# A fused two-block model on one core: product groups opened differently, waits per tile, and three reorderings behind the expert stage

## The chip, the cores and the metric

The kernel runs on 1 core of one Trainium2 chip. Its engines work beside each other: TensorE (PE, matrix products; its weight loads are listed as PEld), VectorE (DVE), ScalarE (ACT), GpSimd (POOL) and SyncE (SP, which here only issues DMAs). They meet by semaphores: an instruction waits until a counter has reached a value. The metric is the time on the device in microseconds, as the median of several runs. All data is fp32, at batch 1, 256 tokens and a model width of 1024.

## The reference

Two blocks one after the other on x (256 x 1024), cut to what matters here:

```python
# first block
z = rmsnorm(x, g_mix) @ w_in                      # pool mixer, short convolution, gates
x = x + m @ w_out
x = x + peer_ffn(rmsnorm(x, g_ffn), ...)          # 8 heads x top 16 of 16384 experts: gathers
x = rmsnorm(x, g_final)
# second block, layer 0 (gated linear attention) and layer 1 (sparse attention)
for i in range(2):
    xn = rmsnorm_2(h, norm_mix[i])
    main = gla_mixer(...) if i == 0 else nsa_mixer(...)
    mo = mem_attention(mq, mem_kv)                # 4 memory heads
    h = h + concatenate([main, mo]) @ w_out[i]
    h = h + conv_ffn(rmsnorm_2(h, norm_ffn[i]), ...)  # up 1024 -> 2 x 2816, convolution over 3 tokens, silu(a) * b, down
return rmsnorm_2(h, final_norm)
```

rmsnorm divides by sqrt(mean(x^2) + 1e-6) and multiplies by a gain per channel.

## The kernel before

Activations lie transposed, 128 channels on the partitions, 8 tiles (k = 0..7) of 256 tokens. One product in the code is 128 x 128 by 128 x 256 and is two fp32 matmul instructions. Products go into four rotating PSUM banks (`bank`) in an order written down in the list GROUPS; `begin` waits until the bank's former user has been taken out by ACT or DVE (`freed`). A second PSUM area, `wide`, is four banks that hold attention scores, the heads' outputs or the FFN's sum. Weights stream through a ring of four slots in SBUF (`wring`): SP issues a load when the group that last used the slot is complete, and `slot` makes PE wait for it. Every engine runs its instructions in the order in which its part of the program is written; nothing reorders them.

What the change and the next sections touch, in the order of the program:

- **Output projection of layer 0, `wout0`.** Four tiles of two output rows, each a sum over eight input tiles, n = 0..7: first the two of the memory heads (`moT`), then six of the attention (`gout`). DVE makes those head by head (L1566 to L1576: a reciprocal, products, a gated product) and counts them in `g_out`, for which PE waits product by product. The loop is `for i in range(4): for n in range(KT): wout0(i, n)`: a tile is finished before the next begins. Each tile is then added to x by DVE (L1267), squared by ACT and folded by POOL (L514) for the norm's mean.
- **FFN, `ffn`, once in each layer.** PE first writes zeros to all of `wide` with four matmuls on a zero tile (L2293), so that every down product can add. Up-projections 0 and 1 take the weighted x before the norm's scale is known (`raw`, L1817); the mean of squares (L1829) is made inside the first, ACT makes the root, DVE the reciprocal into `rstd` (L1136), scales up-projection 0 (L1142) and makes the eight normed tiles hT = x * gain * rstd (`finish`, L1147), then scales up-projection 1. Up-projection 2 and all later ones use hT; PE waits for all eight tiles in front of it (`pe.wait_ge(normed, norms)`). Tiles from 3 on are made with seven products instead of eight, from sums that POOL makes: four of the weights (`weight_sums`, L530 to L535) and, once, four of hT (`hidden_sums`, L543 to L548, waiting for all eight tiles). After up 2, `down(0, 0)` adds the first hidden tile into `wide` (L2354); it waits for DVE's product (L1608). The loop then alternates an up tile and a down tile.
- **Sparse attention of layer 1.** For each pair of heads PE makes scores, DVE adds the bias and takes the maximum (`nsa_max`, L1744), ACT the exponentials (L1045), DVE the probabilities (`nsa_probs`, L1754 to L1763), PE transposes them (L2443), ACT copies the transposes out (`nsa_turned`), PE makes the values. Before the loop DVE makes four maxima and then the probabilities of the first pair. ACT's queue is exponentials 0 to 3, then the copies of transposes 0 and 1, then exponentials 4 and 5.
- **Final norm.** ACT squares x in four pieces, PE makes the mean (L1807), ACT the root (L663), DVE the reciprocal, in place in PSUM (L1117), and eight products with x and the gain (L1121). SP stores two tiles at a time (L489).

## Time and profile before

| | |
|---|---|
| runs, median (lowest to highest of 3) | 1591.55 us (1589.33 to 1594.05) |
| profiled execution | 1592.82 us, its span 1591.0 us |
| busy: PE, DVE, POOL, ACT | 92%, 59%, 38%, 26% |
| mean granted clock of TensorE | 0.989 of full speed |
| mean DMA rate over the span | 264 GB/s |

The span is the time between the first and the last instruction of the profiled execution; the rest of its time lies around it. All rows of the trace belong to that one execution. A row that merges instructions gives start, duration to the end of the last one, engine, line, operation, tiles, shape and count; a bracket at its end says how long the engine had been idle and whose work ended that.

### The profile page before, as it was taken

The numbers are of one execution on the slowest core, as the hardware profiler recorded it, in microseconds if no ns is written. First come the engines' busy times: TensorE is split into PE (matmuls) and PEld (weight loads), VectorE is DVE, ScalarE is ACT, GpSimd is POOL, SyncE is SP. The second block draws the span as 40 slices with busy tenths as digits, with TensorE's granted clock in tenths as the row PEclk, the third lists the DMA queues.
The fourth block names the chain that finished last, engine by engine and source line by source line (L and its number), as shares of the span: only waits on it lengthen the run. The fifth ranks groups of instructions, "written<-read, shape, count | busy, mean of one in ns | idle before, by whom it ended". The sixth has DMA issues, their size and how long they took to land.

```text
span 1591.0 us, 21988 instructions
## 1 busy us (share of the span) xinstructions
PE 1471.1 (92%) x7682; PEld 1100.0 (69%) x7682; DVE 936.5 (59%) x2355; ACT 405.9 (26%) x990; POOL 597.3 (38%) x525
## 2 busy tenths in 40 slices
PE   8999999999899877777789999999999999999997
PEld 6998845555445433222246788999998877899997
DVE  5662587666766776676456833655554235555554
ACT  2110223212222232222214621111112235211122
POOL 4860234334434443344342303555531000455550
PEclk9999999999999999999999999999999999999999
DMA  8465699999999999999996125644534320644441
GB/s 334 160 222 184 234 427 427 427 426 427 427 423 413 425 427 427 427 414 415 426 426 211 68 103 204 231 159 158 164 143 131 106 107 1 225 159 159 158 132 40
DMA packets 63383, 420.63 MB, mean 264 GB/s; under 512 B 7340, under 2 KB 7788, under 8 KB 16812
## 3 DMA queue, kind: packets, MB, share of 16 engines
q0 software_dynamic: 38560, 277.19, 42.0%
q1 hardware_dynamic: 24736, 142.35, 25.2%
q8 instruction: 47, 0.77, 0.2%
q14 instruction: 40, 0.33, 0.1%
HBM read 417.28 MB, written 3.45 MB: 264 GB/s over the span
## 4 chain that ended last, share of the span: by engine, by line
PE 64%; DMA 20%; DVE 5%; issue 5%; POOL 3%; ACT 2%; SPq 0%; POOLq 0%; DVEq 0%
DMA arena<-uv_dram,arena 19%; PE bank L2314 15%; PE wide L2354 10%; PE wide L2109 9%; PE bank L1840 6%; PE bank L1866 5%; PE bank L1959 3%; ACT arena L663 2%; PE bank L1920 2%; POOL arena L503 2%; PE bank L2487 2%; PE bank L1930 2%; PE bank L2282 2%; PE bank L1817 2%; PE bank L2131 1%
## 5 line engine op out<-in xcount | busy, mean ns | idle before, releaser
L2109 PE MATMUL wide<-arena 128*128 128x512 f32 x1024 | 477.9, 614 | 90.7 <-ACT arena L663 90.5
L2109 PEld LDWEIGHTS wide<-arena 128*128 128x128 f32 x1024 | 191.7, 194 | 354.4 <-issue 198.5
L1386 DVE CUSTOM_DVE_ANT_0 arena<-arena,wide 128x1024 f32<-128x1024 f32 x256 | 312.5, 1221 | 189.4 <-DMA arena<-uv_dram,arena 184.3
L503 POOL DMA_INDIRECT arena<-uv_dram,arena x256 | 259.3, 1013 | 405.3 <-PE wide L2109 287.1
L663 ACT ACTIVATE arena<-arena 128x2 f32<-128x2 f32 (+4 forms) x205 | 72.2, 354 | 537.0 <-DVE arena L1386 416.5
L1600 DVE SCALAR_TENSOR_TENSOR arena<-arena,prm 128x255 f32<-128x255 f32 (+1 forms) x152 | 126.0, 850 | 55.6 <-ACT arena L663 55.5
L2354 PE MATMUL wide<-arena,wring 128*128 128x256 f32 x704 | 158.6, 379 | 0.0
L2354 PEld LDWEIGHTS wide<-arena,wring 128*128 128x128 f32 x704 | 130.9, 190 | 16.2
L1634 DVE TENSOR_TENSOR arena<-bank,arena 128x128 f32<-128x128 f32 x266 | 74.0, 290 | 105.1 <-PE bank L2314 101.5
L514 POOL TENSOR_TENSOR arena<-arena 128x512 f32<-128x512 f32 x15 | 20.2, 1350 | 262.3 <-ACT arena L663 261.6
L663 ACT ACTIVATE arena<-bank 128x128 f32<-128x128 f32 (+8 forms) x101 | 40.4, 402 | 285.3 <-PE bank L2314 104.4
L530 POOL TENSOR_TENSOR arena<-wring 128x512 f32<-128x512 f32 x38 | 48.6, 1280 | 158.5 <-PE bank L2314 153.6
L2314 PE MATMUL bank<-arena 128*128 128x128 f32 x912 | 108.0, 275 | 0.0
L2314 PEld LDWEIGHTS bank<-arena 128*128 128x128 f32 x912 | 104.9, 192 | 0.0
L663 ACT ACTIVATE arena<-cst,arena 128x128 f32<-128x128 f32 x256 | 88.8, 393 | 41.2 <-DVE arena L1407 40.2
L1840 PE MATMUL bank<-hT,wring 128*128 128x256 f32 x384 | 85.1, 381 | 2.3 <-DVE hT L1147 2.3
L1840 PEld LDWEIGHTS bank<-hT,wring 128*128 128x128 f32 x384 | 72.3, 190 | 13.3 <-DVE hT L1147 3.1
L2314 PE MATMUL bank<-hT,wring 128*128 128x128 f32 x608 | 80.2, 275 | 0.0
L2314 PEld LDWEIGHTS bank<-hT,wring 128*128 128x128 f32 x608 | 76.9, 192 | 2.0
L663 ACT ACTIVATE arena<-arena,prm 128x256 f32<-128x256 f32 x76 | 41.5, 593 | 113.9 <-DVE arena L1634 113.9
L1817 PE MATMUL bank<-arena,wring 128*128 128x256 f32 x224 | 52.1, 393 | 7.7 <-DMA wring<-win_dram 7.7
L533 POOL TENSOR_TENSOR arena<-arena,wring 128x512 f32<-128x512 f32 x38 | 54.6, 1436 | 0.0
(290 smaller groups left out, 2040.4 us busy)
## 6 DMA issues: line engine op xcount, KB each, us to landing
wring<-ffn_dram SPq DMA_DIRECT2D x43, 1024.0 KB, 5.1
wring<-ffn_dram SPq DMA_DIRECT2D x44, 512.0 KB, 3.5
wring<-win_dram SPq DMA_DIRECT2D x15, 1024.0 KB, 5.2
wring<-wout_dram SPq DMA_DIRECT2D x12, 1024.0 KB, 4.7
wring<-wq_dram SPq DMA_DIRECT2D x5, 1024.0 KB, 7.3
wring<-mix_dram SPq DMA_DIRECT2D x4, 1024.0 KB, 5.3
arena<-uv_dram,arena POOLq DMA_INDIRECT x256, 12.1
wring<-memkv_dram SPq DMA_DIRECT2D x4, 1024.0 KB, 9.3
```

The source lines that it names most:

```text
L503: pool.indirect_dma_start(out=G[:, n % NBUF, :], out_offset=None, in_=a["uv"], in_offset=bass.IndirectOffsetOnAxis(ap=idx[:, u, r:r + 1], ...
L533: TT_(s2, s1, a11, ALU.subtract).then_inc(w_sums, 1)
L663: return nc.scalar.activation(o, i, func, scale=scale, **kw)
L1386: V.tensor_tensor_reduce(out=G[:, n % NBUF, 0:D], in0=G[:, n % NBUF, 0:D], in1=wide[:, 0:2, :].rearrange("p a b -> p (a b)"), scale=1.0, s ...
L1600: return V.scalar_tensor_tensor(out=fy[:, k % 2, c, sh:S], in0=src, scalar=w_, in1=fy[:, k % 2, c, sh:S], op0=ALU.mult, op1=ALU.add)
L1634: V.tensor_tensor(o, own, i, ALU.add).then_inc(joined, 1)
L1817: ins = MM(b[:, m * S:(m + 1) * S], w[:, (m * KT + k) * 128:(m * KT + k + 1) * 128], src[:, k, :], start=k == 0 and m == 0, stop=k == KT - ...
L1840: ins = MM(b[0:rows, m * S:(m + 1) * S], w[:, (m * kt + k) * width:(m * kt + k) * width + rows], src[:, k, :], start=k == 0, stop=k == kt - 1)
L1866: ins = MM(o, a_[:, q * 128:(q + 1) * 128], b_[:, q, :], start=q == 0, stop=q == 3)
L2109: ins = MM(wide[:, 2 + h, :], diag[:, n % 4, e, :], G[:, r % NBUF, D + 512 * h:D + 512 * (h + 1)], start=r % (HEADS * TOPK) == 0, stop=r % ...
L2314: ins = MM(o, a_[:, q * 128:(q + 1) * 128], b_[:, q, :], start=q == 0, stop=q == 3)
L2354: ins = MM(wide[:, m // 2, (m % 2) * S:(m % 2 + 1) * S], w[:, (16 + m) * 128:(17 + m) * 128], fh[:, k % 2, :], start=False, stop=last and ...
```

## The change

Five edits:

1. `wout0`: the products of the two memory tiles (n = 0, 1) of all four output tiles come first, then n = 2..7 of each. PE waits for `g_out` in the first tile only.
2. FFN: the four zeroing matmuls are gone; the first down product (`first=True`) carries the start flag on the first product of each bank. The zero tile in SBUF goes with them.
3. FFN: the wait for all eight normed tiles ahead of up-projection 2 becomes one wait per tile, in its first half.
4. Sparse attention: `nsa_probs(0)` stands between the second and the third maximum in DVE's order.
5. Final norm: the reciprocal goes to `rstd` in SBUF; DVE makes tiles 0 to 4. ACT multiplies tiles 5 to 7 of x with the gain, ahead of the root, and POOL multiplies them with rstd. The stores are five: tiles 0-1, 2-3, 5-6, 4, 7.

A sixth touches one constant: the root of `mean_mix0` gets `eps2` = 1e-12 for `eps`.

```diff
--- before.py
+++ after.py
@@ -149,8 +149,8 @@
         prm = sb("prm", [128, PRM_W])
         memk = sb("memk", [128, 2, 2, S])
         memv = sb("memv", [128, 2, TT, 256])
-        zero = sb("zero", [128, 512], bf16)
         eps = sb("eps", [128, 1])
+        eps2 = sb("eps2", [128, 1])
         rstd = sb("rstd", [128, S])
         AW = 31900
         arena = sb("arena", [128, AW])
@@ -347,6 +347,7 @@
         group_full = sem("group_full")
         freed = {ACT_: sem("freed_by_act"), DVE_: sem("freed_by_dve")}
         zeroed = sem("zeroed")
+        weighted, normed_pool = sem("weighted"), sem("normed_by_pool")
         fence = {e: sem(f"fence_{e}") for e in ("pool", "dve")}
         squared = sem("squared")
         rooted = sem("rooted")
@@ -484,10 +485,11 @@
                         sp.dma_start(wq4[m], a["wq4"][:, m]).then_inc(aside_in, 16)
                 for s in range(0 if name != "win" else slots, slots):
                     load(s, s)
-            for n in range(4):
-                sp.wait_ge(normed, 8 * 10 + 2 * n + 2)
-                sp.dma_start(out[:, 2 * n:2 * n + 2, :], hT[:, 2 * n:2 * n + 2, :]).then_inc(stored, 16)
-            sp.wait_ge(stored, 64)
+            for ks, ready, count in ((slice(0, 2), normed, 82), (slice(2, 4), normed, 84), (slice(5, 7), normed_pool, 2),
+                                     (slice(4, 5), normed, 85), (slice(7, 8), normed_pool, 3)):
+                sp.wait_ge(ready, count)
+                sp.dma_start(out[:, ks, :], hT[:, ks, :]).then_inc(stored, 16)
+            sp.wait_ge(stored, 80)
 
 
         @block.gpsimd
@@ -652,6 +654,10 @@
                                    kvc[64 * base:64 * base + 64, :, 16 * half:16 * half + S - 16]).then_inc(c_moved, 16)
             fold(sqF, 20)
             sums(1, 80)
+            pool.wait_ge(weighted, 3)
+            pool.wait_ge(freed[DVE_], TAKEN[GROUP0["mean_out"]])
+            for k in range(5, KT):
+                nc.gpsimd.tensor_tensor(hT[:, k, :], xgF[:, k, :], rstd[:], ALU.mult).then_inc(normed_pool, 1)
 
 
         @block.scalar
@@ -675,10 +681,10 @@
                     act.wait_ge(wait, at[n])
                     copy(o[:, 2 * n:2 * n + 2, :], i[:, 2 * n:2 * n + 2, :], func=ACT.Square).then_inc(squared, 1)
 
-            def root(stage, i=0, rows=128, n=S):
+            def root(stage, i=0, rows=128, n=S, bias=eps):
 
                 b = full(stage, i)[0:rows, 0:n]
-                copy(b, b, func=ACT.Sqrt, bias=eps[0:rows]).then_inc(rooted, 1)
+                copy(b, b, func=ACT.Sqrt, bias=bias[0:rows]).then_inc(rooted, 1)
 
 
             act.preload_act_table(ACT.Sqrt)
@@ -841,7 +847,7 @@
             for k in range(KT):
                 act.wait_ge(added, 7 + k // 4)
                 both(1, k).then_inc(sq_done, 1)
-            root("mean_mix0")
+            root("mean_mix0", bias=eps2)
 
             def expo(J):
                 layer, kind, h, tt = JOBS[J]
@@ -1094,6 +1100,8 @@
             ffn("ffn1", 1)
             act.preload_act_table(ACT.Sqrt)
             square(sqF, xT, added, [21, 22, 23, 24])
+            for k in range(5, KT):
+                copy(xgF[:, k, :], xT[:, k, :], scale=P("final_norm", k)).then_inc(weighted, 1)
             root("mean_out")
 
 
@@ -1147,11 +1155,11 @@
                     V.scalar_tensor_tensor(out=dst[:, k, :], in0=src[:, k, :], scalar=col[:, k:k + 1], in1=rstd[:],
                                            op0=ALU.mult, op1=ALU.mult).then_inc(normed, 1)
 
-            V.memset(zero[:], 0.0).then_inc(zeroed, 1)
             for z in zp:
                 V.memset(z[:, :, 0:16], 0.0).then_inc(zeroed, 1)
             V.memset(cu[:, :, 0:2], 0.0).then_inc(zeroed, 1)
             V.memset(eps[:], EPS).then_inc(zeroed, 1)
+            V.memset(eps2[:], EPS * EPS).then_inc(zeroed, 1)
             dve.wait_ge(g_mix_in, 16)
             for k in range(KT):
                 dve.wait_ge(x_in[k // 4], 16)
@@ -1764,9 +1772,11 @@
                     ins.then_inc(n_p, 1)
 
             dve.wait_ge(late, LATE)
-            for J in range(4):
-                nsa_max(J)
+            nsa_max(0)
+            nsa_max(1)
             nsa_probs(0)
+            nsa_max(2)
+            nsa_max(3)
             for Q in range(len(NSA) // 2):
                 if 2 * Q + 2 < len(NSA):
                     nsa_probs(Q + 1)
@@ -1779,7 +1789,8 @@
             finish(hT, xT, P("norm_ffn", 8, 8))
             scale("ffn1", 1)
             ffn("ffn1", 1)
-            norm("mean_out", xT, [(hT, "final_norm", 0)])
+            inverse("mean_out")
+            finish(hT, xT, P("final_norm", 0, 8), range(5))
 
 
         @block.tensor
@@ -2272,7 +2283,7 @@
                 if n == 0:
                     begin("wout0", i)
                     slot("wout0", i)
-                if k < 6:
+                if k < 6 and i == 0:
                     pe.wait_ge(g_out, k + 1)
                 b = bank[(GROUP0["wout0"] + i) % 4]
                 w = wring[:, (SLOT0["wout0"] + i) % RING, :]
@@ -2284,19 +2295,20 @@
                     done(ins)
 
             for i in range(4):
-                for n in range(KT):
+                for n in range(2):
+                    wout0(i, n)
+            for i in range(4):
+                for n in range(2, KT):
                     wout0(i, n)
 
             def ffn(stage, layer, norms, gains, mean):
                 g0, n0, k0 = GROUP0[stage], SLOT0[stage] - layer, layer * FT
-                for n in range(4):
-                    MM(wide[:, n, :], zero[:, 0:128], zero[:], start=True, stop=False)
                 def up(j, mean=None):
                     b = begin(stage, j)
                     if layer and j == 0:
                         pe.wait_ge(front1_in, 16)
                     w = front1 if layer and j == 0 else slot(stage, j - layer)
-                    done(raw(w, xgF, b, gains, mean) if j < 2 else project(w, hT, b))
+                    done(raw(w, xgF, b, gains, mean) if j < 2 else project(w, hT, b, norms=norms - 8))
 
                 def up_seven(j, k):
 
@@ -2346,13 +2358,13 @@
                     earlier = sum((SLOT0["ffn0"] + s) % RING == r for s in range(FT)) if layer else 0
                     return 16 * (earlier + k // RING + 1)
 
-                def down(j, k, last=False):
+                def down(j, k, first=False, last=False):
                     pe.wait_ge(f_hid, j + (k0 + 1))
                     pe.wait_ge(d_full[(n0 + k) % RING], down_loads(k) if isinstance(j, int) else up_seven.i * 16 + down_loads(k))
                     w = wring[:, (n0 + k) % RING, :]
                     for m in range(KT):
                         ins = MM(wide[:, m // 2, (m % 2) * S:(m % 2 + 1) * S], w[:, (16 + m) * 128:(17 + m) * 128],
-                                 fh[:, k % 2, :], start=False, stop=last and m % 2 == 1)
+                                 fh[:, k % 2, :], start=first and m % 2 == 0, stop=last and m % 2 == 1)
                         if last and m % 2:
                             ins.then_inc(f_sum, 1)
                     if not last:
@@ -2360,9 +2372,8 @@
 
                 up(0, mean)
                 up(1)
-                pe.wait_ge(normed, norms)
                 up(2)
-                down(0, 0)
+                down(0, 0, first=True)
                 for j in range(PLAIN, 6):
                     up_seven(j, j)
                     down(j - 2, j - 2)
@@ -2372,7 +2383,7 @@
                         up_seven(i * 4 + (s + 6), s + 6)
                         down(i * 4 + (s + 4), s + 4)
                 down(FT - 2, FT - 2)
-                down(FT - 1, FT - 1, True)
+                down(FT - 1, FT - 1, last=True)
 
             ffn("ffn0", 0, 56, 16, ("mean_f0", sqF, 12))
             for i in range(2):
```

PE's order around `wout0`; bank2, bank3, bank0 and bank1 are the four output tiles, gla_out is `g_out`, w_full the ring's loads. Before:

```order
L1840 MATMUL bank1<-hT,wring 128x256 x15
L2282 MATMUL bank2<-arena,wring 128x256 [waits w_full3,freed_by_act]
L2282 MATMUL bank2<-arena,wring 128x256 x3
L2282 MATMUL bank2<-arena,wring 128x256 [waits gla_out]
L2282 MATMUL bank2<-arena,wring 128x256
```

After:

```order
L1851 MATMUL bank1<-hT,wring 128x256 x15
L2293 MATMUL bank2<-arena,wring 128x256 [waits w_full3,freed_by_act]
L2293 MATMUL bank2<-arena,wring 128x256 x3
L2293 MATMUL bank3<-arena,wring 128x256 [waits w_full0,freed_by_act]
L2293 MATMUL bank3<-arena,wring 128x256 x3
L2293 MATMUL bank0<-arena,wring 128x256 [waits w_full1,freed_by_act]
L2293 MATMUL bank0<-arena,wring 128x256 x3
L2293 MATMUL bank1<-arena,wring 128x256 [waits w_full2,freed_by_act]
L2293 MATMUL bank1<-arena,wring 128x256 x3
L2293 MATMUL bank2<-arena,wring 128x256 [waits gla_out]
```

The memory products of tiles two to four, with their waits for ring slot and bank, now stand ahead of the first wait for a head.

PE's order around the third up-projection of layer 0 (`bank<-hT,wring` behind `bank<-arena,wring`, up-projection 1). Before:

```order
L1817 MATMUL bank<-arena,wring 128x256 [waits gained]
L1817 MATMUL bank<-arena,wring 128x256
L1840 MATMUL bank<-hT,wring 128x256 [waits w_full1,freed_by_dve,normed]
L1840 MATMUL bank<-hT,wring 128x256 x15
L2354 MATMUL wide<-arena,wring 128x256 [waits d_full3,ffn_hidden]
L2354 MATMUL wide<-arena,wring 128x256 x7
```

After:

```order
L1828 MATMUL bank<-arena,wring 128x256 [waits gained]
L1828 MATMUL bank<-arena,wring 128x256
L1851 MATMUL bank<-hT,wring 128x256 [waits normed,w_full1,freed_by_dve]
L1851 MATMUL bank<-hT,wring 128x256 [waits normed] x7
L1851 MATMUL bank<-hT,wring 128x256 x8
L2366 MATMUL wide<-arena,wring 128x256 [waits d_full3,ffn_hidden]
L2366 MATMUL wide<-arena,wring 128x256 x7
```

The one wait for `normed` became eight, on the products of the first output row; the down product stands where it was.

DVE's order at the start of the sparse attention; a maximum is the ISA rows of 128x128 or 128x256, the probabilities begin with the 128x4 TENSOR_SCALAR that waits for nsa_exp. Before:

```order
L1744 ISA arena<-wide,arena 128x256
L1744 ISA arena 128x1
L1744 ISA arena<-wide,arena 128x256 [waits nsa_scores]
L1744 ISA arena 128x1
L1744 ISA arena<-wide,arena 128x256
L1744 ISA arena 128x1
L1754 TENSOR_SCALAR arena<-arena 128x4 [waits nsa_exp]
L1756 RECIPROCAL arena<-arena 128x4 [waits dve_steps]
L1759 TENSOR_TENSOR arena<-arena 128x4 [waits dve_steps]
L1763 TENSOR_SCALAR arena<-arena 128x128 [waits dve_steps]
```

After:

```order
L1752 ISA arena<-wide,arena 128x128
L1752 ISA arena 128x1
L1762 TENSOR_SCALAR arena<-arena 128x4 [waits nsa_exp]
L1764 RECIPROCAL arena<-arena 128x4 [waits dve_steps]
L1767 TENSOR_TENSOR arena<-arena 128x4 [waits dve_steps]
L1771 TENSOR_SCALAR arena<-arena 128x128 [waits dve_steps]
L1771 TENSOR_SCALAR arena<-arena 128x128 x3
L1752 ISA arena<-wide,arena 128x256 [waits nsa_scores]
```

The first probabilities moved ahead of the two maxima of 256 columns, behind the second of 128.

## Rows read from the trace of the kernel before

**Rows 1.** The page's first part: busy us, share of span, instructions.

```profile
PE 1471.1 (92%) x7682; PEld 1100.0 (69%) x7682; DVE 936.5 (59%) x2355; ACT 405.9 (26%) x990; POOL 597.3 (38%) x525
```

**Rows 2.** The chain that ended last: start us, us, engine, line, count.

```profile
1361.32 5.18 PE bank L1817 x24
```

**Rows 3.** The timeline of wout0, 944 to 1000: start, us, engine, line, operation.

```profile
950.76 4.48 PE L2282 MATMUL bank<-arena,wring 128*128 128x256 f32 x20
...
950.95 0.33 SPq L428 DMA_DIRECT2D wring<-wout_dram  x1
...
956.98 0.87 DVE L1576 SCALAR_TENSOR_TENSOR arena<-arena,prm 128x256 f32<-128x256 f32 x2
...
957.12 25.26 PE L2282 MATMUL bank<-arena,wring 128*128 128x256 f32 x108 [1.88 <-DVE arena L1572]
...
982.22 1.03 PE L2293 MATMUL wide<-zero 128*128 128x512 bf16 x4
```

**Rows 4.** Window: us; PE, PEld, DVE, ACT, POOL busy; clock, DMA share, GB/s.

```profile
958.30:961.70 3.40, 3.40 (x10) 2.68 (x9) 0.23 (x1) 0.00 (x0) 0.00 (x0) 0.51 0.00 0
```

**Rows 5.** DMA issues from 930 to 1000: count, KB each, median us to landing.

```profile
wring<-wout_dram SPq DMA_DIRECT2D x3, 1024.0 KB, 4.7
...
arena<-turned_dram POOLq DMA_DIRECT2D x1, 1536.0 KB, 15.2
```

**Rows 6.** The timeline of the first FFN's norm, 985 to 1012.

```profile
989.13 8.80 PE L1817 MATMUL bank<-arena,wring 128*128 128x256 f32 x40
...
998.80 7.17 PE L1840 MATMUL bank<-hT,wring 128*128 128x256 f32 x32 [0.88 <-DVE hT L1147]
...
1001.20 0.43 DVE L1608 TENSOR_TENSOR arena<-arena 128x256 f32<-128x256 f32 x1 [0.16 <-ACT arena L663]
...
1002.84 1.28 POOL L548 TENSOR_TENSOR arena<-hT,arena 128x512 f32<-128x512 f32 x1
...
1005.82 3.62 PE L2354 MATMUL wide<-arena,wring 128*128 128x256 f32 x16
```

**Rows 7.** The timeline of the second FFN's norm, 1345 to 1400.

```profile
1360.30 1.03 PE L2293 MATMUL wide<-zero 128*128 128x512 bf16 x4
...
1361.16 5.34 PE L1817 MATMUL bank<-arena 128*128 128x256 f32 x24
...
1363.72 1.34 POOL L514 TENSOR_TENSOR arena<-arena 128x512 f32<-128x512 f32 x1 [0.21 <-ACT arena L663]
...
1368.93 7.07 PE L1817 MATMUL bank<-arena,wring 128*128 128x256 f32 x32
...
1370.35 6.97 DVE L1147 SCALAR_TENSOR_TENSOR hT<-xT,prm,rstd 128x256 f32<-128x256 f32 x8
...
1377.38 7.17 PE L1840 MATMUL bank<-hT,wring 128*128 128x256 f32 x32 [1.38 <-DVE hT L1147]
```

**Rows 8.** The timeline of the sparse attention's start, 1290 to 1312.

```profile
1297.53 0.44 PE L2443 MATMUL wide<-cst,arena 128*128 128x128 f32 x2 [2.56 <-DVE arena L1763]
...
1297.70 0.19 ACT L1045 ACTIVATION_READ_ACCUMULATOR arena<-arena 128x1 f32 x1
...
1298.01 0.39 ACT L663 ACTIVATE arena<-wide 128x256 f32<-128x256 f32 x1
```

**Rows 9.** The timeline of the final norm, 1574 to 1592.

```profile
1580.17 0.63 ACT L663 ACTIVATE arena<-xT 128x512 f32<-128x512 f32 x1 [0.23 <-DVE xT L1673]
...
1582.83 0.45 ACT L663 ACTIVATE bank<-bank,eps 128x256 f32<-128x256 f32 x1 [2.03 <-PE bank L1807]
...
1585.21 3.22 DVE L1121 SCALAR_TENSOR_TENSOR hT<-xT,prm,bank 128x256 f32<-128x256 f32 x8
```

**Rows 10.** Single lines: duration ns min/median/max, first and last start us.

```profile
L1147 DVE SCALAR_TENSOR_TENSOR hT<-xT,prm,rstd x24: 471/479/2687, 992.3 to 1376.9; 128x256 f32<-128x256 f32 x24
...
L620 POOL TENSOR_TENSOR arena<-arena x6: 724/728/746, 831.8 to 853.2; 128x256 f32<-128x256 f32 x6
...
L489 SPq DMA_DIRECT2D out_dram<-hT x4: 332/338/348, 1586.1 to 1588.5; - x4
```

## The prediction

> **What bounds the kernel now.** First the page's busy line: TensorE (PE) works 92% of 1591.0 us, VectorE (DVE) 59% [rows 1]. Outside the expert stage, where gathers end the waits, time is therefore PE's work and the gaps in it. Then the chain that ended last: behind the expert stage it stays on PE almost without a break; its row of 24 matmul instructions in 5.18 us gives the measure used below, 0.216 us for an instruction of 256 columns at the full clock, 0.432 for a product of the code (two instructions) [rows 2]. Then the timeline at each place that the change names; there the reader is to look for brackets, the time for which an engine stood idle and whose work ended that: DVE's head products in wout0 [rows 3], DVE's norm in both FFNs [rows 6, 7], DVE's probabilities in the sparse attention [rows 8], and at the very end no gap but a string of short steps one after another [rows 9]. For each I ask what PE waits for, and what is late next.
>
> **Part 1, output projection of layer 0 (wout0): -3.8 us.** The stage's first instruction starts at 950.76; after 20 of them PE stands still for 1.9 us for DVE's fourth head, and 108 more follow from 957.12. The zeroing matmuls behind them start at 982.22 [rows 3]. That is 31.46 us for 128 instructions, which at 0.216 take 27.65. The 3.8 us over are the wait and, just behind it, a stretch from 958.3 to 961.7 with a granted clock of 0.51 (the 1.2 GHz level) and only 10 instructions in 3.4 us [rows 4]: PE had stood still, then the clock fell.
> The change puts the memory products of all four tiles, 32 instructions, in front: 950.76 + 32 x 0.216 = 957.67. DVE's last head products end at 957.85 [rows 3]; PE needs heads five and six only four products later, so it waits for none. Next to be late is a load: SP issues the fourth tile's at 950.95, such loads land after 4.7 us in the median [rows 3, 5], at 955.65, and PE now asks after 24 instructions, at 955.94, with 96 instructions queued behind that wait. The margin is 0.3 us. The first FFN tile's load is released when the first tile is complete, now at 957.67 + 12 x 0.432 = 962.9, and needed at 978.4: harmless. Bounds: 0 (the load 3.8 us late) to 3.8; without a clock fall in the run compared with, 2.2. I take 3.8.
>
> **Part 2, zeroing matmuls: -1.7 us.** Four of them set the next matmul from 1360.30 to 1361.16, 0.86 us; layer 0 has the same four [rows 3, 7]. There PE has work before and behind. In layer 1 the next to be late is the sum of squares: the GpSimd's (POOL) last fold ends at 1363.72 + 1.34 = 1365.06, and PE reaches the mean at 1360.30 + 24 x 0.216 = 1365.48 [rows 7]: 0.4 us to spare. The first down product opens its bank by a flag, at no instruction. Bounds 0.9 to 1.7.
>
> **Part 3, waits per tile: -2.7 us.** In layer 0 the second up-projection ends at 989.13 + 40 x 0.216 = 997.77 and the third starts at 998.80, when the eighth normed tile is out [rows 6]; in layer 1, 1368.93 + 32 x 0.216 = 1375.84 against 1377.38 [rows 7]. That is 1.0 and 1.5 us, and 0.1 each, my estimate, for a slower first pair. Per tile PE needs one tile each 0.43 us. Counted back from the eighth by 0.48 us, the median of such a product [rows 10], the first tile is out by 995.4 and 1373.9: ahead of PE, also with Part 2's 0.86 us in front. Then comes the down product: its hidden tile is done at 1001.20 + 0.43, and PE comes to it at 1005.82 [rows 6], now about 2 us earlier, with 2 us to spare. POOL's hidden sums still wait for all eight tiles; they end at 1002.84 + 1.28 = 1004.1 and are wanted behind the down product, 1005.82 + 3.46 = 1009.3 less the same 2 us [rows 6]. Bounds 0 (given back at the next wait) to 2.7.
>
> **Part 4, sparse attention, probabilities ahead of two maxima: 0.** PE waits 2.56 us, from 1294.97 to 1297.53, for the probabilities of heads one and two, which stand behind the maxima of heads three and four in DVE's queue [rows 8]. Ahead of them they are done before PE asks, and its first transposes move forward by 2.5 us. But the second transposes need ScalarE (ACT) to have copied the first out, and in ACT's queue the exponentials of heads three and four stand before that copy. They start from the same maxima, whose scores do not move, and end at 1297.70 + 0.19; the copy runs at 1298.01 [rows 8]. ACT's order is untouched, so 0.1 us is won and I count nothing. The other end is the whole wait, -2.5.
>
> **Part 5, final norm on two engines: +0.4 us.** ACT's three scalings go in front of the root, which waits for PE until 1582.83. Its last square ends at 1580.17 + 0.63 = 1580.80, and if a scaling took as long as that square of twice its width, three would end at 1582.7 [rows 9]: hidden. From 1585.21 DVE makes eight products in 3.22 us; the last store is issued at 1588.5, 3.3 us after the start [rows 9, 10]. After the change DVE makes five, POOL three, of 0.73 in the nearest row of this shape [rows 10]. Were the engines independent, POOL's third would end after 2.3 us, and the last two stores (0.34 each on SP) go out at 2.5 and 2.8: -0.5. But DVE's norm products in the FFNs, whose multiplier lies in SBUF as it will here, take up to 2.69 us for 0.48 [rows 10] while POOL adds. In layer 1 eight took 6.97 us beside POOL's four weight sums [rows 7], against 3.22 in the final norm, with the multiplier in PSUM and POOL idle: 0.94 us more per POOL instruction of 512 columns, so I estimate 0.47 for 256. 5 x 0.40 + 3 x 0.47 = 3.4, and the last store stands behind one more issue: 3.7 against 3.3. I take these +0.4; strictly one after the other, 5 x 0.40 + 3 x 0.73 = 4.2 and an issue make +1.3.
> The Trainium skill ("SBUF — State Buffer", section "Who interferes with whom") says that a DVE instruction with two SBUF inputs and a GpSimd instruction reading SBUF each hold a shared interface for their whole length and block the other. The stretched products agree with it; taken strictly it gives the +1.3, and 1585.9 us in place of 1585.0.
>
> The rest (another constant for one root, a memset fewer while DVE waits for its first load) lies beside other work.
>
> **Sum.** -3.8 - 1.7 - 2.7 + 0 + 0.4 = -7.8. The profiled execution took 1592.82 us (the span and 1.8 around it), so 1585.0. It lies 1.27 above the median of the runs, 1591.55, which differ by up to 4.7. From the median it is 1583.7 if that run had the slow-clock stretch too, 1585.3 if not. I take 1584.6.
>
> **Rivals.**
> *Part 4 wins its wait.* For it: PE's longest single wait behind the expert stage, by name for the work that moves. Against it: the copy behind two exponentials. -2.5: 1582.1; chance 0.09.
> *Part 3 wins nothing*, another engine setting the start of the steady loop. For it: DVE and POOL both work without a pause around 1000 us. Against it: the 2 us to spare. +2.7: 1587.3; chance 0.14.
> *The clock falls elsewhere.* PE's idle time in the sparse attention is cut in two and all later idle pieces shift; a fall costs the 1.6 us of Part 1 (3.8 less 2.2), and Part 1's own may be missing from the run compared with. Two of these: 1587.8; chance 0.13.
> *Slower: the fourth wout0 load is late.* PE stops before 96 instructions and pays one for one from 955.94 on. To turn the sign it must take 5.0 + 7.8 = 12.8 us from its issue; the slowest load near it, on POOL's queue, took 15.2 [rows 5]. That long, and with a clock fall after the stop: 1584.6 + 10.2 + 1.6 = 1596.4. Against it: 4.7 us in the median. Chance 0.03.
> *My forecast*: 0.61.
>
> About 0.3%, 4.8 us, is what a measurement here can tell from no change, so faster means below 1586.8. Of the forecast 0.59 lies there, of Part 4's rival 0.09, of the two middle ones 0.10: 0.78. Slower 0.03, the rest, 0.19, within. The range goes from Part 4's gain less some of the scatter of runs, 1580.5, to the middle ones, 1588.2.
>
> **What would show it.** Right: no idle bracket on PE in wout0 and about 27.7 us for it; no matmul on the zero tile; the third up-projection directly behind the second; the first transposes of the sparse attention at once, the second still behind ACT; DVE products of over 0.5 us beside POOL in the final norm, and the last store no earlier than 3.3 us after the reciprocal. Wrong: PE waiting for a ring load in wout0, or for the hidden tile, or a granted clock of 0.5 behind the expert stage.

## The result: slower, 1599.6 us for 1592.3

The changed kernel took 1599.61 us in the median of 8 runs, beside it the kernel before 1592.30 us, also of 8: a ratio of 1.0063, 95% interval 1.0045 to 1.0081. Predicted were 1584.6 us and faster. The runs lie in two groups, five from 1597.04 to 1599.80 us (mean granted clock 0.988 to 0.991) and three from 1607.83 to 1608.45 (0.983 to 0.985); those of the kernel before lie from 1589.33 to 1594.47. So there are two things to explain: some 6 us more in all runs, and some 9 more in three of them.

The profile after is of the fastest run. The page's head answers to [rows 1]:

```profile
span 1595.2 us, 21976 instructions
PE 1466.1 (92%) x7674; PEld 1097.5 (69%) x7674; DVE 936.9 (59%) x2352; ACT 407.1 (26%) x993; POOL 600.1 (38%) x528
```

The chain of the changed kernel, in order of time (start, us, what), at the places of [rows 2, 3, 6 and 7]:

```profile
849.32 7.15 PE wide L2120 x16
...
961.67 27.63 PE bank L2293 x128
...
995.34 8.63 PE bank L1828 x40
1003.98 6.91 PE bank L1851 x32
...
1371.11 8.63 PE bank L1828 x40
1379.74 6.91 PE bank L1851 x32
...
1571.07 10.36 PE wide L2366 x48
```

And the same four places in the chain of the kernel before:

```profile
838.56 7.15 PE wide L2109 x16
...
998.80 7.17 PE bank L1840 x32
...
1377.38 7.17 PE bank L1840 x32
...
1568.98 10.36 PE wide L2354 x48
```

Read the differences of the starts, place by place. At the end of the expert stage the changed kernel is already 10.76 us late (849.32 against 838.56). At the third up-projection of layer 0 it is 5.18 late, at that of layer 1 2.36, at the last down products 2.09; and it ends 4.2 later (span 1595.2 against 1591.0). So behind the expert stage the edits win 8.7 us (Parts 1 to 4 were to win 8.2), the tail gives 2.1 back, and before all that 10.8 us are lost in a stage that no edit names. What the gathers did there, in the window from 210 to 840 us (the DMA view: what was moved, then the gathers' count and their median us from issue to landing). Before:

```profile
DMA packets 36616, 265.78 MB, mean 422 GB/s; under 512 B 4065, under 2 KB 4193, under 8 KB 4193
arena<-uv_dram,arena POOLq DMA_INDIRECT x244, 12.1
```

After:

```profile
DMA packets 36119, 262.18 MB, mean 416 GB/s; under 512 B 4007, under 2 KB 4135, under 8 KB 4135
arena<-uv_dram,arena POOLq DMA_INDIRECT x244, 12.4
```

They move 1.4% less in the same 630 us, while the share of time in which the DMA engines are busy is 1.01 in both: the stage is bound by them. In the trace the 17th gather is issued at 219.0 us before and 219.7 after, the 193rd at 668.5 and 676.7: one each 2.554 us, and each 2.596 after, 1.6% more. The last of the 256 goes out 10.4 us later (828.7, 839.2), so nearly the whole 10.8 us are theirs.

**Theory A.** The diff takes away a tile of 1024 B per partition and adds one of 4 B, which takes 32. The tiles behind them move: in the built programs the arena starts at byte 100864 before, a multiple of 512, and at 99872 after, 32 over a multiple of 256. The gathers write their rows of 8 KB per partition into a buffer 49152 B inside the arena, so each row now begins 32 B off. Rival B: a changed instruction, or the runs' scatter.

### The profile page after: what moved, and what is told of

The parts are those of the page before. It is cut to its first block, busy times and chain, and to the rows that moved or that the text cites. A ratio compares the mean times of both kernels' runs of the same rounds, so it can differ in the third digit from the quotient of the medians.

```text
span 1595.2 us, 21976 instructions
## 1 busy us (share of the span) xinstructions
PE 1466.1 (92%) x7674; PEld 1097.5 (69%) x7674; DVE 936.9 (59%) x2352; ACT 407.1 (26%) x993; POOL 600.1 (38%) x528
## 4 chain that ended last, share of the span: by engine, by line
PE 65%; DMA 21%; issue 5%; POOL 3%; DVE 3%; ACT 2%; SPq 0%; POOLq 0%; DVEq 0%
DMA arena<-uv_dram,arena 20%; PE bank L2326 15%; PE wide L2366 10%; PE wide L2120 9%; PE bank L1851 6%; PE bank L1877 4%; PE bank L1970 3%; PE bank L1828 3%; POOL arena L505 2%; PE bank L1931 2%; PE bank L2293 2%; ACT arena L669 2%; PE bank L2498 2%; PE bank L1941 2%; PE bank L2142 1%
## 5 line engine op out<-in xcount | busy, mean ns | idle before, releaser
L1394 DVE CUSTOM_DVE_ANT_0 arena<-arena,wide 128x1024 f32<-128x1024 f32 x256 | 312.5, 1221 | 201.7 <-DMA arena<-uv_dram,arena 197.0
```

The costliest lines, as they stand in the source:

```text
L1394: V.tensor_tensor_reduce(out=G[:, n % NBUF, 0:D], in0=G[:, n % NBUF, 0:D], in1=wide[:, 0:2, :].rearrange("p a b -> p (a b)"), scale=1.0, s ...
```

## Experiments on the gathers' buffer

**The changed kernel, arena moved back.**

```diff
         rstd = sb("rstd", [128, S])
+        pad = sb("pad", [128, 248])
         AW = 31900
```

> The changed kernel with an unused tile of 992 B per partition ahead of the arena: the arena starts at byte 100864 again, as in the kernel before (99872 in the changed kernel, 32 over a multiple of 256). Theory A (the expert stage is slow because its gathers now write rows that start 32 B off): DMA in the expert stage back to about 427 GB/s in the slices, the stage about 10.7 us shorter than in the changed kernel, and the whole at about 1584 to 1586 us, a ratio of about 0.995 to the kernel before. Theory B (a changed instruction or the runs' scatter, not the address): about 1597 to 1600 us, about 420 GB/s, like the changed kernel.

Measured: eight runs from 1586.14 to 1589.67 us, four from 1596.59 to 1597.68; profiled span 1584.3. I call it the aligned kernel. Its ratio over all runs, 0.9993 (0.9975 to 1.001), is that of a mixture.

**The kernel before, arena moved by 32 and by 64 B** (a tile of [128, 8], or [128, 16], at the same place).

> The kernel before with an unused tile of 32 B per partition ahead of the arena: the arena, and with it the gathers' rows, starts 32 B later, at 100896. Theory A: about 420 GB/s in the expert stage and about 10.7 us more, 1603 us, a ratio of about 1.007. Theory B: as before, 1592 us and 427 GB/s.

Measured: 1604.36 us, ratio 1.0073 (1.0060 to 1.0086).

> The kernel before with an unused tile of 64 B per partition ahead of the arena (arena at 100928, 64 over a multiple of 256). Theory A with a step of 256 B (each 8 KB row takes one transfer more as soon as it does not start on a multiple of 256 B): about 1603 us, 420 GB/s. Theory A with a step of 64 B: 1592 us, 427 GB/s. Theory B: 1592 us.

Measured: 1602.46 us, ratio 1.0070 (1.0053 to 1.0087).

**The changed kernel, only the gathers' buffer moved.**

```diff
         scores = take(UNITS, 2 * NKEYS)
+        free["at"] += 56
         G = take(NBUF, 2 * D)
```

> The changed kernel, its arena left at 99872, with 224 B left free inside it just ahead of the gather buffer: only that buffer and the small tiles behind it move, the buffer to byte 149248, a multiple of 256 and not of 512. Theory A, gathered rows alone, step of 256 B or less: about 1585 us, 427 GB/s. Theory A with a step of 512 B: about 1598 us. Rival A2 (the engines' own reads and writes in the shifted arena are slow, not the gathers' writes): about 1598 us, since nearly all other tiles stay shifted.

Measured: six runs from 1586.54 to 1589.11 us, six from 1596.63 to 1597.60.

The DMA row of each in the same window. The aligned kernel:

```profile
DMA packets 36630, 265.89 MB, mean 422 GB/s; under 512 B 4066, under 2 KB 4194, under 8 KB 4194
```

The kernel before with 32 B:

```profile
DMA packets 36111, 262.14 MB, mean 416 GB/s; under 512 B 4005, under 2 KB 4133, under 8 KB 4133
```

The kernel before with 64 B:

```profile
DMA packets 36221, 262.89 MB, mean 417 GB/s; under 512 B 4023, under 2 KB 4151, under 8 KB 4151
```

The changed kernel with the buffer alone moved:

```profile
DMA packets 36628, 265.87 MB, mean 422 GB/s; under 512 B 4066, under 2 KB 4194, under 8 KB 4194
```

Theory A holds, both ways round: 32 B make the kernel before as slow as the changed one, and moving the buffer alone, with nearly all else in the arena left 32 B off, gives the rate back; so it is the gathers' rows and not the engines' reads of other tiles. Their reads of the gathered rows move with the buffer, but DVE's product with such a row takes 1221 ns in the mean of the window in all six traces, so these are not it either. 64 B over a multiple of 256 is about as bad as 32; an odd multiple of 256 is good. 128 wasn't tried.
The Trainium skill ("DMA: Bandwidth & Descriptors", section "How a descriptor splits into AXI transactions") says that a descriptor, one contiguous piece of a DMA, which starts on a multiple of 256 B is cut into transfers of 256 B, and that one which doesn't has its first transfer begin at the boundary below. It says this of reads; for an 8 KB row it would be 33 transfers in place of 32. These runs agree with it for writes into SBUF in the step of 256 B (32 and 64 slow, 0 and 256 not); by the count of transfers it would be 3% (an estimate from that page), and 1.6% per gather was measured.

## Experiments on the second group of runs

The profile of the kernel with the buffer moved is of the upper group, that of the aligned kernel of the lower. TensorE at the same place in both, the window view (stretch, us and busy time of PE with its instructions, then granted clock, DMA share and GB/s). The aligned kernel:

```profile
1209.00:1216.20 7.20, 7.20 (x36) 1.00 0.80 233
1216.20:1219.80 3.60, 3.60 (x35) 1.00 1.04 280
1219.80:1239.70 19.90, 19.90 (x131) 1.00 0.35 127
```

With the buffer alone moved:

```profile
1209.00:1216.20 7.20, 7.20 (x35) 1.00 0.77 228
1216.20:1219.30 3.10, 3.10 (x29) 0.99 1.01 253
1219.30:1239.70 20.40, 20.40 (x87) 0.50 0.25 85
```

For 20.4 us the clock stands at 0.50 (the 1.2 GHz level), and TensorE, busy all the time, does 87 instructions where the other does 131 in half a microsecond less. That is a loss of about 10 us (20.4 x 0.5), about the distance of the groups. I call it the long fall. That a run without a profile has it is inferred, below too, from its time (9 to 10 us above the lower group) and its mean granted clock. It isn't the fall of [rows 4], which came behind a stop: here nothing stopped. My first theory, C, was that just this brings it on: the edits leave no pause in TensorE's work. Its rival, D, was that it comes by chance in any kernel of this kind.

**The aligned kernel with one edit undone, and the kernel before with one edit.** The first: wout0 tile by tile again, with its waits.

```diff
-                if k < 6 and i == 0:
+                if k < 6:
                     pe.wait_ge(g_out, k + 1)
...
             for i in range(4):
-                for n in range(2):
-                    wout0(i, n)
-            for i in range(4):
-                for n in range(2, KT):
+                for n in range(KT):
                     wout0(i, n)
```

> The changed kernel with its arena on a multiple of 256 B again (as in the run before of that name) and the first edit undone: wout0 tile by tile, with its waits for the heads. The runs of the aligned kernel fell in two groups, 8 near 1587.6 us with a mean granted clock of 0.989 or more, and 4 near 1597 us at 0.984; in a profile of the upper kind the clock stands at 0.5 for 20.5 us from 1219.4 on, in the gated attention of layer 1, after TensorE had worked without a stop since the expert stage. Theory C (that long fall comes because nothing interrupts TensorE any more between the expert stage and there; the stop in wout0 with its short fall prevented it): no run in the upper group, all at 1587.6 + 3.8 = about 1591.4 us (or + 2.2 where the short fall stays away). Rival D (the long fall comes by chance in any kernel of this kind, wout0 has nothing to do with it): again about one run in three 9 to 10 us above the others.

Measured: all five runs from 1599.73 to 1601.78 us, clock 0.979 to 0.984. Neither theory expected that. The profile has the stop in wout0, a granted clock of 0.50 just behind it as in [rows 4], and the long fall all the same:

```profile
958.14 25.26 PE L2294 MATMUL bank<-arena,wring 128*128 128x256 f32 x108 [1.88 <-DVE arena L1581]
```

Theory C fell here.

The second: the third up-projection waits for all eight normed tiles.

```diff
-                    done(raw(w, xgF, b, gains, mean) if j < 2 else project(w, hT, b, norms=norms - 8))
+                    done(raw(w, xgF, b, gains, mean) if j < 2 else project(w, hT, b))
...
                 up(1)
+                pe.wait_ge(normed, norms)
                 up(2)
```

> The aligned changed kernel with the third edit undone: the third up-projection of both FFNs waits for all eight normed tiles at once. By the prediction's step 2.7 us slower than the aligned kernel without long fall, about 1590 us; by its rival (given back at the next wait) 1587.6 us. Theory C says of the long fall: TensorE then stops for about 1.0 us near 993 us; if a stop of that size is enough, no run in the upper group, and if only a stop with a fall of the clock prevents it, about one in three.

Measured: six runs from 1589.41 to 1593.81 us, median 1590.9, and six from 1600.12 to 1601.33. The third edit's price shows in the brackets of the two up-projections, idle time and what ended it:

```profile
995.67 7.17 PE L1852 MATMUL bank<-hT,wring 128*128 128x256 f32 x32 [1.30 <-DVE hT L1156]
...
1376.25 7.17 PE L1852 MATMUL bank<-hT,wring 128*128 128x256 f32 x32 [1.71 <-DVE hT L1156]
```

3.0 us together, and the lower group is 3.3 us above that of the aligned kernel (1587.6); the step said 2.7.

The third: the final norm on VectorE alone, four stores.

```diff
-            inverse("mean_out")
-            finish(hT, xT, P("final_norm", 0, 8), range(5))
+            norm("mean_out", xT, [(hT, "final_norm", 0)])
```

(and without ScalarE's three scalings and GpSimd's three products).

> The aligned changed kernel with the fifth edit undone: the final norm's eight products on VectorE again, four stores. In the aligned kernel's trace the end came 7.9 us after the first product, against 5.8 in the kernel before: the last store is issued 4.5 us after it (3.3 before), and GpSimd's last drain ends 0.7 us after all else. Theory (the fifth edit costs 2.1 us, of which GpSimd's drain is 0.7): about 1585.5 us in the lower group. By the prediction's +0.4: 1587.2 us. The long falls, about one in three, stay by theory C and by D.

Measured: seven runs from 1583.49 to 1587.66 us, median 1584.8, and five from 1594.58 to 1596.03. The lower group is 2.8 us below that of the aligned kernel (1587.6).

The fourth: the kernel before with the new wout0 alone (the first diff of this section turned round).

> The kernel before with the first edit alone: the memory heads' products of all four wout0 tiles in front, no waits behind the first tile. By the prediction 2.2 to 3.8 us faster than the kernel before, about 1589.5 us. Theory C: TensorE then works from the expert stage to the first FFN without a stop, but the stop of 1.0 us for the third up-projection is still there; long falls (runs near 1599 us, clock 0.984) come if a stop of 1 us without a fall does not prevent them. Rival D: they come as rarely as in the kernel before (none in 31 runs).

Measured: five runs from 1588.15 to 1591.40 us, seven from 1599.16 to 1600.12. The lower group's median, 1590.83, is about 2 us below the kernel before, close to the 2.2 of the bound without a clock fall.

So the long fall belongs to no single edit: it stays with each of these three undone, and it comes with the first alone (the second and the fourth were not tried by themselves), while the kernel before has it in 3 of the 84 runs beside these experiments. What the kernels share is that TensorE gets to that place at another time. In both profiles with a long fall that there were then, the clock goes down in the same place, while or just when 32 matmul instructions of 36 columns end: the sparse attention's gates of layer 1. With the buffer alone moved these instructions run from 1216.25 to 1220.37 us. In the kernel with wout0's old order, the timeline and the window view:

```profile
1221.19 3.66 PE L2396 MATMUL bank<-wring,arena 128*128 128x36 f32 x32
1224.78 1.97 PE L2205 MATMUL wide<-memk,arena 64*128 64x256 f32 x8
```

```profile
1221.20:1224.90 3.70, 3.70 (x35) 1.00 0.99 265
1224.90:1245.40 20.50, 20.50 (x84) 0.50 0.20 73
```

Theory E is that this narrow stretch itself brings the clock down, and that it does so or not by the moment at which it comes; rival F, that the load ahead of it does.

**The gates shared out** (in the aligned kernel without its fifth edit): half of the narrow products go between the wide ones ahead.

```diff
-            done(project(slot("nsamq", 0), xn1, b, norms=56))
+            project(wq_, xn1, bq, tiles=1, norms=56, width=128)
...
+            for k in range(KT):
+                ins = MM(bq[:, S:2 * S], wq_[:, (KT + k) * 128:(KT + k + 1) * 128], xn1[:, k, :], start=k == 0, stop=k == KT - 1)
+                if k < KT - 1:
+                    gate_part(0, k)
+            done(ins)
+            gate_part(0, KT - 1)
+            for k in range(KT):
+                ins = gate_part(1, k)
             done(ins)
```

> The aligned changed kernel with its fifth edit undone (final norm on VectorE) and one new edit: the gate products of layer 1, 32 matmul instructions of 36 columns that stand in one stretch of 3.66 us, are shared out: half of them go between the wide products just ahead, half stay behind these (about 1.8 us in one stretch). In the two profiles with a long fall (TensorE's clock 0.5 for 20.5 us) the fall begins right at the end of that stretch or within it. Theory C has fallen: the kernel with wout0's old order had the long fall in all its runs, and that with wout0's new order alone in 7 of 12. Theory E (the narrow stretch itself brings the clock down, and only when it lies just so against the moments at which the clock is set; the edits moved it there by coming to it some us earlier): no run in the upper group, all at 1583.5 to 1587.7 us as the lower group of the kernel without this edit. Rival F (the long fall comes from the load TensorE had before, whatever stands there): again about four runs in ten near 1595 us.

Measured: 1586.98 us, five runs from 1585.04 to 1587.89, ratio 0.9968 (0.9955 to 0.9981). It beats both kernels, the one before by 0.3%. In the trace the mixing (7 of 16 narrow products) costs nothing: from the up-projection ahead of it to the products of 68 columns behind it the chain takes 20.10 us (1201.84 to 1221.94), in the aligned kernel 20.09 (1200.82 to 1220.91). By the times this isn't shown: the median is 2.1 us above the lower group of the kernel without the mixing (1584.8), in another set of runs. Five runs without a long fall, where 5 of 12 had one, are little evidence by themselves; the last experiment has more.

**The kernel before, delayed** by more zeroing matmuls ahead of the first FFN:

```diff
+                for n in range(0 if layer else 16):
+                    MM(wide[:, n % 4, :], zero[:, 0:128], zero[:], start=True, stop=True)
```

> The kernel before with 16 more zeroing matmuls ahead of the first FFN, 3.46 us of TensorE's time, of which 1.03 us lie beside the wait for the normed tiles: the gate products of layer 1 come 2.4 us later than in the kernel before. Their 3.66 us then begin, by the place they have in the profile of the kernel before against the steps in which the clock is set, about where they begin in the profile in which every run had the long fall. Theory E: most or all runs with a long fall, 1593 + 2.4 + 9.5 = about 1605 us, clock 0.984. Rival F: none or one, about 1595.4 us.

Measured: two runs at 1596.84 and 1598.59 us, four from 1604.72 to 1606.57. The upper four are where E put them; the lower two are some 2 us above what was expected without a long fall. In its profile the narrow products begin at 1224.43, and the clock:

```profile
1224.40:1227.80 3.40, 3.40 (x32) 1.00 0.99 286
1227.80:1248.30 20.50, 20.50 (x86) 0.50 0.19 72
```

> The same with 10 more zeroing matmuls, 2.16 us, so a delay of 1.1 us. Theory E: the narrow stretch begins in the middle of a step of the clock, as in the kernels before with a moved arena, which had no long fall in 10 of 11 runs: 1594.1 us and few or no long falls. Rival F: as the kernel before, 1594.1 us. Only together with the run of 2.4 us does it tell something: by E the two differ, by F they don't.

Measured (10 in place of 16): six runs from 1591.91 to 1594.68 us, six from 1602.20 to 1605.10. A miss: E expected few. A delay alone brings the long fall, which F did not expect either, but the place that the stretch has in one profile doesn't tell how often.

**The narrow stretch doubled, and shared out where all runs fell.**

```diff
-            for t in range(TT):
+            for t in (0, 1, 0, 1):
```

> The kernel before with the gate products of layer 1 done twice over, one pass behind the other into the same place: the stretch of narrow products is 7.3 us long in place of 3.66. [...] Rival F: 2 long falls in 69 runs of the kernel before, so none or one here; about 1596 us.

Theory E had a long fall in every run, at about 1606 us. Measured: all four runs from 1607.98 to 1609.24 us, clock 0.981 to 0.984, some 3 us more than that. In the profile the doubled stretch, 64 instructions, runs from 1223.09 to 1231.53, and the clock goes down in its middle:

```profile
1223.00:1228.80 5.80, 5.80 (x54) 1.00 0.88 251
1228.80:1249.40 20.60, 20.60 (x92) 0.50 0.16 52
```

The second is the kernel with wout0's old order and the gates shared out as above.

> The kernel with all edits but the first (wout0 in its old order), which had a long fall in all five of its runs at 1601.3 us, with the gate products of layer 1 shared out as in the run before of that name. Theory E: no run with a long fall, 1601.3 - 9.6 = about 1591.7 us. Rival F: long falls in all runs, about 1601 us.

Measured: all eleven runs from 1589.03 to 1592.88 us, median 1589.86; unshared it was 1601.26 in the median of five, all with a long fall. In the profile the clock stays up over the mixed stretch and behind it:

```profile
1217.10:1223.80 6.70, 6.70 (x49) 1.00 0.77 197
1223.80:1244.30 20.50, 20.50 (x133) 1.00 0.38 148
```

The first half of theory E holds in both directions, and F fails in both: with the same wide work ahead, a longer narrow stretch gives the long fall in 4 of 4 runs (3 of 84 without), a shared-out one in 0 of 11 (5 of 5 without). The second half, that the moment at which the stretch comes decides, is not shown: the two delays point that way, and the forecast for the shorter one missed.

## Why the prediction was wrong

**The step that failed** is the last sentence of the change: "The rest (another constant for one root, a memset fewer while DVE waits for its first load) lies beside other work." It priced the removed tile by its memset, at nothing, and not by what its 1024 B held in place: the address of the buffer that the gathers of the DMA-bound expert stage write to. That is +10.8 us, more than all gains together, and it was not among the rivals. The one slower rival, a late load in wout0, did not occur.

**The clock.** The rival "the clock falls elsewhere" looked for falls behind idle time and priced one at 1.6 us. The one that came stood in work without a gap and cost 9 to 10 us; by their times and clocks 3 of the 8 runs of the changed kernel had it, and the profiled one did not. Without it the change would still have been slower: the median of the lower group is 1598.6, 14 us above the forecast.

**Part 1, wout0:** right. The chain has 128 instructions in 27.63 us without a break (predicted 27.65). Up to the third up-projection of layer 0, Parts 1 to 3 were to win 3.8 + 0.86 + 1.1 = 5.8 us; they won 10.91 - 5.18 = 5.7, where 10.91 is how late wout0 starts (961.67 in place of 950.76). As predicted, a part of it was the short fall of the run compared with: the kernel before with Part 1 alone wins about 2. (The prediction's own rows give 2.0 for the wait, 957.12 less 950.76 + 20 x 0.216, and 1.8 for the fall, not 2.2 and 1.6.)

**Parts 2 and 3, layer 1:** 0.86 + 1.6 were predicted. In the aligned kernel the third up-projection starts at 1368.84, 8.54 us earlier than before; 6.29 of these it had at the projections ahead of the sparse attention, which leaves 2.25. About 0.3 more came in each FFN behind that start, where the 32 instructions take 6.91 us in place of 7.17; 0.1 was my estimate for this.

**Part 4, sparse attention:** right. The timeline of the changed kernel where [rows 8] stood:

```profile
1299.50 0.44 PE L2454 MATMUL wide<-cst,arena 128*128 128x128 f32 x2
...
1302.40 0.36 ACT L669 ACTIVATE arena<-wide 128x256 f32<-128x256 f32 x1
...
1302.90 0.41 PE L2454 MATMUL wide<-cst,arena 128*128 128x128 f32 x2 [1.06 <-ACT arena L669]
```

The first transposes run at once; the second still wait for the copy that stands behind ACT's exponentials. In the aligned kernel the second ones come 6.55 us earlier than before, and all work already came 6.29 earlier: 0.26 won, 0.1 forecast.

**Part 5, final norm:** wrong in size, 2.1 for +0.4. The timeline of the changed kernel's end, for [rows 9]:

```profile
1587.30 3.47 DVE L1155 SCALAR_TENSOR_TENSOR hT<-xT,prm,rstd 128x256 f32<-128x256 f32 x5
1587.40 2.69 POOL L660 TENSOR_TENSOR hT<-arena,rstd 128x256 f32<-128x256 f32 x3 [30.29 <-DVE rstd L1144]
1588.67 3.53 SPq L491 DMA_DIRECT2D out_dram<-hT  x5
```

And of the aligned kernel with Part 5 undone:

```profile
1580.06 3.22 DVE L1123 SCALAR_TENSOR_TENSOR hT<-xT,prm,bank 128x256 f32<-128x256 f32 x8
1580.96 2.68 SPq L491 DMA_DIRECT2D out_dram<-hT  x4
```

The four stores behind the first (the timeline again), and DVE's five products (the line view: shortest, median and longest in ns):

```profile
1590.40 1.80 SPq L491 DMA_DIRECT2D out_dram<-hT  x4
L1155 DVE SCALAR_TENSOR_TENSOR hT<-xT,prm,rstd x5: 473/941/948, 1587.3 to 1590.3; 128x256 f32<-128x256 f32 x5
```

The cost has three parts.

- *The products*, 3.47 us for 3.22. Beside POOL's products three of DVE's five take 0.94 us, and from start to start 0.86 in place of 0.40: 0.46 more each, which is the 0.47 that I had estimated, and 3.47 for the 3.4 of the sum. POOL's take 0.9 each, not the 0.73 of the nearest row. That the two engines hold each other up agrees with the Trainium skill's rule on the shared interface ("SBUF — State Buffer", section "Who interferes with whom"); its strict reading, which gave the bound of +1.3, is not borne out: one after the other the products would have taken 4.2.
- *The stores.* SP's last issue ends 4.9 us after the first product, against 3.6: 1.3 us, as large as that bound, but by luck, since 1.1 of it lie behind the products. This is the term that was mis-sized: "one more issue" behind the last product. SP takes its stores in order. The second waits for DVE's fourth product until 1590.40, though the third, of POOL's tiles, had its data at 1589.2. Then four go out in a row until 1592.20, three of them after the last product at 1590.77, one each 0.39 to 0.49 us where 0.34 was reckoned.
- *The end*, which I had not counted. From SP's last issue to the end of the span it is 3.0 us with Part 5 (1592.20 to 1595.23) and 2.2 without (1583.64 to 1585.82). In the trace GpSimd's closing drain ends 0.23 us before the span does and 0.7 after SP's; in the kernel before SP's is the last. That this drain is the 0.8 us is read from the trace and wasn't tried by itself.

The runs give somewhat more, 2.8 us between the lower groups with and without Part 5.

Without the address and the long fall the sum was nearer, but not right: the lower group of the aligned kernel has 1587.6 us where 1584.6 were forecast, and Part 5, 2.1 to 2.8 us for +0.4, is most of the difference. The profiled run of 1586.1 us, against 1585.0 in the sum for a profiled run, looks better than this because it is the fastest of its group.

## What to carry to other kernels

When a tile is added or removed, work out where every later tile lands, and put buffers that DMAs fill at full rate on a multiple of 256 B on purpose. Price an edit in a kernel's last microseconds by the whole tail: the stores that still stand in the queue, in their order, and what each engine has to do to finish. Where runs fall in two groups, take a profile of each and compare the granted clock stretch by stretch: here it was a stretch of narrow products, and mixing half of them with wide ones took the fall away, at no cost that the trace shows.

## What the runs showed of the hardware

- While 8 KB rows were gathered into SBUF (210 to 840 us), DMA moved 422 GB/s in the mean where the rows began on a multiple of 256 B, and 416 or 417 where they began 32 or 64 B past one.
- TensorE's granted clock fell from 1.00 to 0.50 for 20.4 to 20.5 us while it was busy without a gap, at or just before the end of 32 matmul instructions of 36 columns in about 3.7 us, and in the middle of 64 of them. In which share of runs it does that differs from kernel to kernel (by their times and clocks): 3 of 84 in the kernel before, 4 of 12 in the aligned one, 5 of 5 with wout0's old order, 0 of 11 with that order and the narrow instructions shared out. A delay of 1 to 2 us on the way changes the share (6 of 12, 4 of 6); what fixes it for one run stays open.
- The kernel before with its arena 32 or 64 B off comes to that place 8 to 12 us later, and 10 of its 11 runs had no long fall; the one at 1609.76 us (clock 0.987) wasn't profiled.
